# The update of the samples' matrix states moves from the mixer to GpSimd, beside the FFN and the experts

## The chip, the cores and the metric

The kernel runs on one core of a Trainium2 chip. Times are device microseconds of one execution of the whole program. Engines are named TensorE (PE in the rows), VectorE (DVE), ScalarE (ACT), GpSimd (POOL) and SyncE (SP, which here only issues weight loads).

## The reference, cut to what matters

It is one inference step of a two-layer decoder for a prompt of 256 tokens and for 8 samples of one new token each. A layer is a mixer (one input projection, an HGRN2 group with 4 heads of 128x128 state and an RG-LRU group, one output projection) and a channel mixer: a dense SwiGLU in layer 0, top-2-of-8 experts in layer 1. The part that the change touches is the state of the samples. For one token and each head the reference comes down to

```python
f = lb + (1 - lb) * sigmoid(fz)          # forget gate, one per key row
k = (1 - lb) * sigmoid(-fz)              # key
S_new[k_row, :] = f[k_row] * S[k_row, :] + k[k_row] * v[:]
o = q @ S_new
```

`S_new` is an output of the program (8 samples, 4 heads, 128x128, per layer: 2 MB). The output `o` is computed as `(q*f) @ S + (q.k) * v`, from the old state, so nothing after the mixer needs `S_new`.

## The kernel before, in words

Every engine has its own program, written in the order in which it runs; semaphores join them. There is no scheduler. All 264 tokens (256 and 8) are the columns of tiles, features are the partitions. Buffers share places by hand (`at(name, offset, ...)`).

Weights come in units of 1 MB (`raw`, 6 slots, loaded by SyncE when slot u-6 has been split). ScalarE rounds a unit to `w_hi` (`hi`, L487), VectorE makes the rest `w_lo` (`lo`, L788), each with 3 slots; TensorE multiplies three times per piece (`mm3`, L1358 to L1360). This pipeline runs through everything: 12 units of the input projection, 4 of the output projection, 33 of the FFN (11 steps of 3), and per expert 7 steps of 6 units.

In a mixer, after the input projection, the engines work on a chain: gates (L1450, L589), decay factors (L602, L607), then on VectorE `cum`, `zx`, `lev` (L1021, L1023, L1039), the scans (L1041), the copy of the heads' outputs from PSUM (L1048) and the samples' own term (L1049). From there, one branch goes on through the square (L628), sums on TensorE (L1508), Ln and Exp (L632, L633), `zf` (L1075) and the gating of four heads (L1077) to `m_hi` and `m_lo` (L622, L1069); the other is the RG-LRU's (L1054 to L1063), whose four chunks are merged first. The output projection takes the chunks in the order 4 to 7, 0 to 3, and VectorE adds each of its 8 columns of output to `xT` (L1093).

The samples' states: ScalarE issues the load of `hstate` (L555) behind the input projection, since it lies where `h_hi` and `h_lo` lie. TensorE reads it (L1486, 32 products of one column). GpSimd multiplies it by the forget gate (L412, eight instructions of 128x512). The value row of a sample has to reach all 128 partitions: GpSimd makes diagonal matrices of its high and low part (`v_diag`, L424, sixteen instructions), TensorE multiplies them by ones (`spread_value`, L1500, two matmuls per sample), and VectorE adds key times the PSUM row to the decayed state (`new_state`, L1033, four per sample). Two samples are handled before the output projection, and one behind each of its first six columns. GpSimd then stores the 2 MB (L428). `norm_hi` on ScalarE (L523) waits for that store before it writes `h_hi` of the next norm; in layer 1 VectorE waits for it before the router's work.

In the expert stage GpSimd only gathers the next expert's tokens (L449, an indirect DMA), once per expert.

Of the kernel before, what the change touches and what calls it, by code (L numbers as in the profile page):

```python
# [42 lines left out]
STATES_FIRST = 2  # L43
# [29 lines left out]
def trunk(nc, x_prompt, x_sample, state_hgrn, state_lru, state_conv, norm1_g, w_in, lower_bounds,  # L73
# [5 lines left out]
    with ctx:  # L79
# [14 lines left out]
        def end(name):  # L94
# [15 lines left out]
        small = at("small", end("rw"), [168])  # L110
# [21 lines left out]

        v_diag = [at("v_diag0", end("v_tok"), [2, HEADS, P], F32R),
                  at("v_diag1", end("key"), [2, HEADS, P], F32R)]
# [7 lines left out]
        vs = at("vs", end("outs_t"), [2, HEADS, NSAMPLE], F32R)  # L142
# [27 lines left out]
        rt = at("rt", HH, [16, 3, EXPERTS])  # L170
# [3 lines left out]
        y_rows = at("y_rows", end("hF"), [3, D])  # L174

        ps = ctx.enter_context(nc.psum_tensor("ps", [P, 8, 512], F32))
        h_dram = nc.dram_tensor("h_rows_scratch", [T, D], F32, kind="Internal").ap()

# [11 lines left out]
        tmp = small[:, 48:160]  # L190

# [22 lines left out]
        gelu_ready, vs_high, vs_split = sem("gelu_ready"), sem("vs_high"), sem("vs_split")  # L214
# [6 lines left out]
        st_landed, st_decayed, diag_ready = sem("st_landed"), sem("st_decayed"), sem("diag_ready")  # L221
        kv_done, st_new, st_stored = sem("kv_done"), sem("st_new"), sem("st_stored")
# [124 lines left out]
        def _(pool):  # L347
# [49 lines left out]
            for l in range(DEPTH):  # L397
# [17 lines left out]
                pool.wait_ge(fin_done, l + 1)  # L415
                pool.wait_ge(vs_split, l + 1)
                for b in range(NSAMPLE):
                    if b == 1:
                        pool.wait_ge(om_ready, l + 1)
                    if b >= 2:  # L420
                        pool.wait_ge(kv_done, NSAMPLE * l + b - 1)
                    for part in range(2):
                        v_b = vs[:, part, :, b:b + 1].bitcast(F32).broadcast_to([P, HEADS, P])
# [19 lines left out]
            pool.wait_ge(st_stored, 16 * DEPTH)  # L443
            pool.wait_ge(fin_stored, 16 * DEPTH)
            pool.wait_ge(rows_stored, 16 * (1 + 4 * DEPTH))
# [6 lines left out]

            pool.wait_ge(h_stored, 16 * 3)
            pool.wait_ge(idx_ready, 1)
            gather_rows()
            pool.wait_ge(blocks_ready, 1)
            nb = pool.value_load(blocks_i[0:1, 0:1], min_val=1, max_val=3)
            with pool.Fori(0, nb) as b:
                with pool.Fori(0, EXPERTS) as e:
                    it = b * EXPERTS + e  # L460
                    pool.wait_ge(idx_ready, it + 2)
                    pool.wait_ge(gathered, it * 2 + 2)
                    pool.sem_inc(gather_begun, 1)
                    gather_rows()
# [4 lines left out]
        def _(act):  # L469
# [1346 lines left out]
```

## Time and profile before

| | |
|---|---|
| runs | 1667.12, 1672.84, 1673.19 us; median 1672.84 |
| profiled execution | 1667.08 us, its span 1665.4 us |
| TensorE busy | 1551.2 us, mean granted clock 0.961 |
| VectorE busy | 1302.6 us |
| ScalarE busy | 963.2 us |
| GpSimd busy | 116.5 us |
| DMA | 438.9 MB, mean 264 GB/s |

The profile is of one execution. Busy shares are of the whole span; its stages are the first mixer (to about 208 us), the FFN (to 395), the second mixer (to 600), the router (to 630) and the experts (to 1640). PEclk is the clock that TensorE was granted, as a part of 2.4 GHz: 0.5 is 1.2 GHz.

### The profile page before, as it was taken

What the parts mean: (1) busy time and instruction counts of PE and PEld (TensorE: products, weight loads), DVE (VectorE), ACT (ScalarE), POOL (GpSimd) and SP (SyncE); (2) the same over time, 40 slices, a digit from 0 to 9 for tenths busy, and PEclk for the clock granted to TensorE, in tenths of its full rate; (3) what the DMA queues carried; (4) which work ended last, traced back from release to release, by engine and by line L of the source; (5) the groups of instructions that cost most, each with busy time, mean ns of one, the idle gap of its engine ahead of it and who ended that gap; (6) DMA issues with size and microseconds to landing.
All of it is one profiled execution on the core that took longest, in us unless ns stands there. A gap on an engine that the chain in (4) does not pass through costs nothing.

```text
span 1665.4 us, 23819 instructions
## 1 busy us (share of the span) xinstructions
PE 1551.2 (93%) x8538; PEld 1332.5 (80%) x8538; DVE 1302.6 (78%) x1244; ACT 963.2 (58%) x800; POOL 116.5 (7%) x104
## 2 busy tenths in 40 slices
PE   6986899999897677999999999999999999999996
PEld 5985799999897676888888888888888888888884
DVE  5786656666667747889889889889889889889886
ACT  4434343334534316677677677677677677677672
POOL 2024400000002610000000000000000000000000
PEclk9996999999999678999999999999999999999999
DMA  8451444445334036999999999999999999999990
GB/s 272 158 162 36 134 147 166 167 165 187 128 127 127 15 105 252 334 378 351 339 376 355 338 382 345 339 380 349 340 373 354 338 376 346 344 379 354 336 360 26
DMA packets 214524, 438.88 MB, mean 264 GB/s; under 512 B 7248, under 2 KB 62984, under 8 KB 214480
## 3 DMA queue, kind: packets, MB, share of 16 engines
q1 hardware_dynamic: 208176, 421.59, 71.1%
q0 software_dynamic: 3088, 10.14, 1.9%
q10 hardware_dynamic: 3216, 6.55, 1.3%
q8 instruction: 29, 0.48, 0.1%
q14 instruction: 15, 0.12, 0.0%
HBM read 431.29 MB, written 7.03 MB: 263 GB/s over the span
## 4 chain that ended last, share of the span: by engine, by line
PE 84%; DVE 9%; issue 3%; ACT 2%; DMA 1%; PEld 0%; DVEq 0%; ACTq 0%; SPq 0%; POOLq 0%; PEldq 0%
PE ps L1358 26%; PE ps L1360 25%; PE ps L1359 25%; DVE w_lo L788 2%; PE ps L1402 1%; PE ps L1675 1%; PE ps L1374 1%; DMA out_dram<-hstate 1%; DVE xc L1041 1%; PE ps L1647 1%; DVE xc L949 1%; PE ps L1635 1%; DVE zq L922 1%; DVE sc L937 0%; DVE lev L1077 0%
## 5 line engine op out<-in xcount | busy, mean ns | idle before, releaser
L788 DVE TENSOR_TENSOR w_lo<-raw,w_hi 128x2048 fp32r<-128x2048 f32 x401 | 913.7, 2292 | 189.0 <-ACT w_hi L487 186.6
L487 ACT ACTIVATE w_hi<-raw 128x2048 fp32r<-128x2048 f32 x401 | 762.7, 1917 | 357.9 <-PE ps L1360 207.8
L1358 PE MATMUL ps<-w_hi,xg 128*128 128x512 f32 x896 | 358.1, 400 | 9.9 <-DVE w_lo L788 9.9
L1360 PE MATMUL ps<-w_hi,xg 128*128 128x512 f32 x896 | 351.7, 392 | 0.0
L1359 PE MATMUL ps<-w_lo,xg 128*128 128x512 f32 x896 | 351.6, 392 | 0.0
L1358 PE MATMUL ps<-h_hi,w_hi 128*128 128x264 f32 x736 | 215.9, 293 | 25.1 <-DVE h_lo L815 17.0
L1360 PE MATMUL ps<-h_hi,w_lo 128*128 128x264 f32 x736 | 211.2, 287 | 0.0
L1359 PE MATMUL ps<-h_lo,w_hi 128*128 128x264 f32 x736 | 211.0, 287 | 0.0
L1358 PEld LDWEIGHTS ps<-w_hi,xg 128*128 128x128 f32 x896 | 168.8, 188 | 47.9 <-DVE w_lo L788 14.0
L1360 PEld LDWEIGHTS ps<-w_hi,xg 128*128 128x128 f32 x896 | 168.5, 188 | 37.4
L1359 PEld LDWEIGHTS ps<-w_lo,xg 128*128 128x128 f32 x896 | 169.0, 189 | 33.5
L1358 PE MATMUL ps<-w_hi,gT 128*128 128x512 f32 x448 | 179.4, 401 | 2.2 <-DVE gT L1275 2.2
L1359 PE MATMUL ps<-w_lo,gT 128*128 128x512 f32 x448 | 176.9, 395 | 0.0
L1360 PE MATMUL ps<-w_hi,gT 128*128 128x512 f32 x448 | 176.8, 395 | 0.0
L1358 PEld LDWEIGHTS ps<-h_hi,w_hi 128*128 128x128 f32 x736 | 140.9, 191 | 30.1 <-issue 29.2
L1359 PEld LDWEIGHTS ps<-h_lo,w_hi 128*128 128x128 f32 x736 | 141.7, 193 | 0.0
L1360 PEld LDWEIGHTS ps<-h_hi,w_lo 128*128 128x128 f32 x736 | 140.8, 191 | 0.0
L1358 PEld LDWEIGHTS ps<-w_hi,gT 128*128 128x128 f32 x448 | 84.0, 187 | 27.2 <-DVE w_lo L788 9.3
L1360 PEld LDWEIGHTS ps<-w_hi,gT 128*128 128x128 f32 x448 | 84.0, 187 | 20.4
L1359 PEld LDWEIGHTS ps<-w_lo,gT 128*128 128x128 f32 x448 | 84.1, 188 | 17.9
L449 POOL DMA_INDIRECT xrow<-h_rows_scratch,slot_token x9 | 18.7, 2082 | 966.7 <-DVE slot_token L1202 939.6
L727 ACT ACTIVATE gT<-ps 128x512 fp32r<-128x512 f32 x56 | 33.6, 599 | 75.4 <-PE ps L1675 75.4
(271 smaller groups left out, 1619.0 us busy)
## 6 DMA issues: line engine op xcount, KB each, us to landing
raw<-in_moe_w_dram SPq DMA_DIRECT2D x336, 1024.0 KB, 6.6
raw<-in_ffn_w_dram SPq DMA_DIRECT2D x33, 1024.0 KB, 5.4
raw<-in_w_in_dram SPq DMA_DIRECT2D x24, 1024.0 KB, 5.6
raw<-in_w_out_dram SPq DMA_DIRECT2D x8, 1024.0 KB, 4.9
out_dram<-hstate POOLq DMA_DIRECT2D x2, 2048.0 KB, 12.2
x_rows<-in_x_prompt_dram SPq DMA_DIRECT2D x1, 1024.0 KB
h_rows_scratch<-h_row ACTq DMA_DIRECT2D x2, 512.0 KB
out_dram<-y_rows ACTq DMA_DIRECT2D x2, 512.0 KB
```

Source lines behind the costliest of these rows:

```text
L449: pool.indirect_dma_start(xrow[:, :], None, h_dram[:, :], bass.IndirectOffsetOnAxis(slot_token[:, 0:1], 0)).then_inc(xrow_landed, 16)
L487: act.activation(w_hi[:, s, :], raw[:, r, :], ACT.Copy).then_inc(hi_made, 1)
L727: act.activation(gT[:, 0, :, :].rearrange("p j n -> p (j n)"), ps[:, 2, :], ACT.Copy).then_inc(gT_hi, 1)
L788: dve.tensor_tensor(w_lo[:, s, :], raw[:, r, :], w_hi[:, s, :].bitcast(F32), ALU.subtract).then_inc(split, 1)
L922: dve.tensor_tensor(qv[:, :, :, 1, :], qv[:, :, :, 1, :], wide(0), ALU.mult).then_inc(lev_ready, 1)
L949: link(dve.scalar_tensor_tensor(out=xc[:, j, 0:NPROMPT], in0=zx[:, j, tap:tap + NPROMPT], scalar=v(V_CW + 16 * l + 4 * tap + j), in1=xc[:, ...
L1041: link(dve.tensor_tensor_scan(xc[:, j, 0:NPROMPT], lev[1][:, j, 0:NPROMPT], lev[2][:, j, 0:NPROMPT], 0.0, ALU.mult, ALU.add))
L1358: pe.matmul(out, l_hi, r_hi, start=start, stop=False)
L1359: pe.matmul(out, l_hi, r_lo, start=False, stop=False)
L1360: return pe.matmul(out, l_lo, r_hi, start=False, stop=stop)
L1374: ins = pe.matmul(ps[:, NORM_BANK[n], 0:T], ones[:, :], sq[:, c, :], start=(c == 0), stop=(c == DC - 1))
L1402: ins = pe.matmul(ps[:, 4 + n % 4, P * h:P * h + P], left[:, h, P * c:P * c + P], right[:, h, P * rc:P * rc + P], start=True, stop=True)
```

## The change

In the mixer, GpSimd no longer decays states or makes diagonals, TensorE no longer spreads values and VectorE no longer updates states. Instead:

- TensorE transposes the samples' values to rows (8 x 512 in PSUM), ScalarE copies them to `vrow`, and GpSimd's queue stores them in DRAM (`v_dram`). ScalarE keeps the samples' keys and forget gates in `key_s` and `forget_s` (before, it made `vs`, and VectorE its low part).
- `vrow` lies where the heads' copy is written, so VectorE waits for that store before the copy.
- Layer 0: once the output projection is done, GpSimd loads the old states again to a place of their own (`hstate2`, free in the FFN). Each sample's value row is then read from DRAM into all partitions (`load_value`, 256 KB, three buffers), and GpSimd does three multiplications and additions of 128x512 per sample (`new_state`). The store follows the last one. ScalarE and VectorE wait for it when layer 1's mixer begins.
- Layer 1: `hstate` stays where it is (the router's tables `rt` have moved), and one sample is updated behind each expert's gather. The loop over the first block's experts is written out on GpSimd for this.
- `norm_hi(1)` waits for the state reads (`o_done`) and not for the store.

The operations on the states are in float32 on one engine, where the values came from two parts before.

```diff
-        vs = at("vs", end("outs_t"), [2, HEADS, NSAMPLE], F32R)
+        hstate2 = at("hstate2", end("ff_lo"), [NSAMPLE * HEADS, P])
+        vb = at("vb", end("y_f"), [3, HEADS, P])
...
@@ gpsimd, mixer
-                pool.wait_ge(st_landed, 16 * (l + 1))
-                for b in range(NSAMPLE):
-                    pool.wait_ge(st_read, NSAMPLE * l + b + 1)
-                    f_b = forget[:, :, NPROMPT + b:NPROMPT + b + 1].broadcast_to([P, HEADS, P])
-                    st = hstate[:, HEADS * b:HEADS * (b + 1), :]
-                    pool.tensor_tensor(st, st, f_b, ALU.mult).then_inc(st_decayed, 1)
...
-                        pool.tensor_tensor(v_diag[b % 2][:, part, :, :],
-                                           ident[:, None, :].broadcast_to([P, HEADS, P]), v_b,
-                                           ALU.mult).then_inc(diag_ready, 1)
-                pool.wait_ge(st_new, NSAMPLE * HEADS * (l + 1))
-                pool.dma_start(hgrn_sample[l].rearrange("b h k v -> k (b h) v"), hstate[:, :, :]
-                               ).then_inc(st_stored, 16)
+                pool.wait_ge(vrow_ready, l + 1)
+                pool.dma_start(v_dram[l], vrow[0:NSAMPLE, :]).then_inc(vrow_stored, 16)
...
+            def load_value(l, b):
+                pool.dma_start(vb[:, b % 3, :, :].rearrange("p h v -> p (h v)"),
+                               v_dram[l, b:b + 1, :].broadcast_to([P, HEADS * P])
+                               ).then_inc(vb_landed[b % 3], 16)
+            def new_state(l, b, st):
+                pool.wait_ge(vb_landed[b % 3], 16 * (per_layer * l + b // 3 + 1))
+                link(pool.tensor_tensor(own_v, own_v, wide(key_s), ALU.mult))
+                link(pool.tensor_tensor(own_st, own_st, wide(forget_s), ALU.mult))
+                link(pool.tensor_tensor(own_st, own_st, own_v, ALU.add))
+                if b + 3 < NSAMPLE:
+                    load_value(l, b + 3)
+                if b == NSAMPLE - 1:
+                    pool.dma_start(hgrn_sample[l].rearrange("b h k v -> k (b h) v"), st
+                                   ).then_inc(st_stored, 16)
...
+            mixer(0)
+            pool.wait_ge(y_done, DC)
+            pool.wait_ge(fin_stored, 16)
+            pool.wait_ge(rows_stored, 16 * 5)
+            pool.dma_start(hstate2[:, :, :], state_hgrn[0].rearrange("b h k v -> k (b h) v")
+                           ).then_inc(st_again, 16)
+            pool.wait_ge(st_again, 16)
+            values_begin(0)
+            for b in range(NSAMPLE):
+                new_state(0, b, hstate2[:, :, :])
+            mixer(1)
...
+            for e in range(EXPERTS):
+                gather_expert(e)
+                new_state(1, e, hstate[:, :, :])
@@ scalar
-                if n in (1, 3):
-                    act.wait_ge(st_stored, 16 * ((n + 1) // 2))
+                if n == 1:
+                    act.wait_ge(o_done, 1)
...
+                if l:
+                    act.wait_ge(st_stored, 16 * l)
...
+                    if u == SPLIT + 4:
+                        act.wait_ge(f_made, l + 1)
+                        act.activation(key_s, key[:, :, NPROMPT:T], ACT.Copy).then_inc(kf_ready, 1)
+                        act.activation(forget_s, forget[:, :, NPROMPT:T], ACT.Copy
+                                       ).then_inc(kf_ready, 1)
-                act.activation(vs[:, 0, :, :], zv[:, :, NPROMPT:T], ACT.Copy
-                               ).then_inc(vs_high, 1)
...
+                act.activation(vrow[0:NSAMPLE, :], ps[0:NSAMPLE, 2, :], ACT.Copy
+                               ).then_inc(vrow_ready, 1)
@@ vector
+                if l:
+                    dve.wait_ge(st_stored, 16 * l)
...
-                    for h in range(HEADS):
-                        st = hstate[:, HEADS * b + h, :]
-                        dve.scalar_tensor_tensor(
-                            out=st, in0=ps[:, 5 + b % 3, P * h:P * h + P],
-                            scalar=key[:, h, NPROMPT + b:NPROMPT + b + 1], in1=st,
-                            op0=ALU.mult, op1=ALU.add).then_inc(st_new, 1)
...
+                dve.wait_ge(vrow_stored, 16 * (l + 1))
                 link(dve.tensor_copy(heads[:, :, :], ps[:, 0:4, 0:T]))
@@ tensor
+                for h in range(HEADS):
+                    ins = pe.transpose(ps[0:NSAMPLE, 2, P * h:P * h + P], zv[:, h, NPROMPT:T],
+                                       ident[:, :])
                 ins.then_inc(v_turned, 1)
...
+                pe.wait_ge(vrow_ready, l + 1)
...
-                    for part in range(2):
-                        ins = pe.matmul(ps[:, 5 + b % 3, :], ones_r[:, :],
-                                        v_diag[b % 2][:, part, :, :].rearrange("p h v -> p (h v)"),
-                                        start=(part == 0), stop=(part == 1))
-                    ins.then_inc(kv_done, 1)
```

How the instructions stand on GpSimd in layer 0 before, from the gelu product (`zr`) on; `hstate` is the samples' state, `v_diag` the diagonals:

```order
L405 TENSOR_TENSOR zr<-zr,zf 128x1056 [waits gelu_sig]
L412 TENSOR_TENSOR hstate<-hstate,forget 128x512 [waits st_read,st_landed]
L412 TENSOR_TENSOR hstate<-hstate,forget 128x512 [waits st_read] x7
L424 TENSOR_TENSOR v_diag_80<-ident,vs 128x512 [waits vs_split,fin_done]
L424 TENSOR_TENSOR v_diag_80<-ident,vs 128x512
L424 TENSOR_TENSOR v_diag_81<-ident,vs 128x512 [waits om_ready]
```

The same place in the changed kernel, to the first sample's update; `hstate_110` is `hstate2`:

```order
L409 TENSOR_TENSOR zr<-zr,zf 128x1056 [waits gelu_sig]
L412 DMA v_rows_scratch<-vrow 8x512 [waits vrow_ready]
L414 DMA out_dram<-s_fin 128x4x128 [waits fin_ready]
L418 DMA out_dram<-outs_t 4x128 [waits rows_ready]
L466 DMA hstate_110<-in_state_hgrn_dram 128x32x128 [waits rows_stored,fin_stored,y_done]
L429 DMA vb<-v_rows_scratch 128x512 [waits kf_ready,vrow_stored,st_again]
L447 TENSOR_TENSOR vb<-vb,small 128x512 [waits vb_landed0]
L448 TENSOR_TENSOR hstate_110<-hstate_110,small 128x512 [waits pool_step]
L449 TENSOR_TENSOR hstate_110<-hstate_110,vb 128x512 [waits pool_step]
```

Between the gelu product and the end of the output projection, only DMA issues are left on GpSimd. VectorE in layer 0 before, from the gating of the heads on:

```order
L1077 SCALAR_TENSOR_TENSOR lev_74<-lev_74,vecT,zf 128x264 x3
L1069 TENSOR_TENSOR m_lo<-lev_74,m_hi 128x264 [waits m_hi_made] x4
L1033 SCALAR_TENSOR_TENSOR hstate<-ps,key,hstate 128x128 [waits st_decayed,kv_done]
L1033 SCALAR_TENSOR_TENSOR hstate<-ps,key,hstate 128x128 x3
L788 TENSOR_TENSOR w_lo<-raw,w_hi 128x2048 [waits hi_made]
L1089 COPY outs_t<-ps 80x128 [waits rows_turned]
```

And in the changed kernel:

```order
L1107 SCALAR_TENSOR_TENSOR lev_74<-lev_74,vecT,zf 128x264 x3
L1099 TENSOR_TENSOR m_lo<-lev_74,m_hi 128x264 [waits m_hi_made] x4
L828 TENSOR_TENSOR w_lo<-raw,w_hi 128x2048 [waits hi_made]
L1117 COPY outs_t<-ps 80x128 [waits rows_turned]
L1121 TENSOR_TENSOR xT<-xT,ps 128x264 [waits y_done] x4
```

The state updates between the low parts, and behind each addition to `xT`, are gone.

## Rows read from the trace of the kernel before

**Rows 1.** The page: a group of instructions, and two kinds of transfers (landing in us).
```profile
L788 DVE TENSOR_TENSOR w_lo<-raw,w_hi 128x2048 fp32r<-128x2048 f32 x401 | 913.7, 2292 | 189.0 <-ACT w_hi L487 186.6
...
raw<-in_moe_w_dram SPq DMA_DIRECT2D x336, 1024.0 KB, 6.6
...
out_dram<-hstate POOLq DMA_DIRECT2D x2, 2048.0 KB, 12.2
```

**Rows 2.** Stages: length, PE, PEld, DVE, ACT, POOL busy (x); clock, DMA share, GB/s.
```profile
112.00:165.00 53.00, 32.08 (x202) 28.69 (x200) 38.71 (x55) 25.34 (x40) 19.15 (x13) 0.75 0.32 99
165.00:195.00 30.00, 27.69 (x182) 26.14 (x183) 23.65 (x51) 8.45 (x9) 14.56 (x13) 0.87 0.20 62
...
210.00:395.00 185.00, 179.93 (x1446) 177.95 (x1446) 111.63 (x130) 71.44 (x56) 0.00 (x0) 0.99 0.50 166
...
630.00:1640.00 1010.00, 1000.40 (x4565) 812.84 (x4566) 878.90 (x585) 710.99 (x475) 17.68 (x8) 1.00 0.96 347
```

**Rows 3.** GpSimd: timeline (start, us), and the tile of diagonals (ns min/median/max, first and last start).
```profile
118.63 2.47 POOL L405 TENSOR_TENSOR zr<-zr,zf 128x1056 f32<-128x1056 f32 x1 [12.21 <-ACT zf L576]
141.84 12.27 POOL L412 TENSOR_TENSOR hstate<-hstate,forget 128x512 f32<-128x512 f32 x8 [20.74 <-PE ps L1486]
166.67 4.89 POOL L424 TENSOR_TENSOR v_diag<-ident,vs 128x512 fp32r<-128x512 f32 x4 [8.14 <-PE ps L1500]
...
L424 POOL TENSOR_TENSOR v_diag<-ident,vs x32: 1042/1050/1756, 154.1 to 582.5; 128x512 fp32r<-128x512 f32 x32
```

**Rows 4.** VectorE beside GpSimd's work, layer 0: timeline, and two lines of tile queries.
```profile
142.38 1.62 DVE L1021 TENSOR_TENSOR cum<-lev 128x1056 f32<-128x1056 f32 x1 [4.29 <-ACTq L609]
144.04 1.98 DVE L1023 SCALAR_TENSOR_TENSOR zx<-cum,zx 128x1056 f32<-128x1056 f32 x1
147.24 1.81 DVE L1039 TENSOR_TENSOR lev<-lev,zx 128x1056 f32<-128x1056 f32 x1 [1.22 <-ACT zx L617]
154.93 1.26 DVE L1048 COPY lev<-ps 128x1056 f32<-128x1056 f32 x1
156.48 1.08 DVE L1054 TENSOR_TENSOR xc<-vecT,lev 128x32 f32<-128x32 f32 x1
166.56 4.09 DVE L1077 SCALAR_TENSOR_TENSOR lev<-lev,vecT,zf 128x264 f32<-128x264 f32 x4
...
L1041 DVE TENSOR_TENSOR_SCAN xc<-lev,lev x8: 1352/1354/1418, 149.1 to 548.9; 128x256 f32<-128x256 f32 x8
...
L1069 DVE TENSOR_TENSOR m_lo<-lev,m_hi x8: 421/422/1272, 170.6 to 568.1; 128x264 fp32r<-128x264 f32 x8
```

**Rows 5.** VectorE where GpSimd is idle, layer 0: timeline.
```profile
123.56 0.21 DVE L967 TENSOR_TENSOR small<-vecT 128x32 f32<-128x32 f32 x1
132.09 1.25 DVE L1016 TENSOR_TENSOR zg<-zg,cum 128x1056 f32<-128x1056 f32 x1
204.79 1.30 DVE L809 SCALAR_TENSOR_TENSOR hF<-xT,vecT,rstd 128x264 f32<-128x264 f32 x3
```

**Rows 6.** TensorE in the second half of layer 0's mixer: timeline.
```profile
140.66 9.30 PE L1486 MATMUL ps<-zq,hstate 128*128 128x1 f32 x64
157.78 3.89 PE L1508 MATMUL ps<-zf,ones 128*128 128x264 f32 x8 [7.81 <-ACT zf L628]
171.90 0.39 PE L1358 MATMUL ps<-m_hi,w_hi 128*128 128x264 f32 x1 [2.02 <-DVE m_lo L1069]
```

**Rows 7.** The chain in layer 1's output projection: start, us, what.
```profile
577.51 0.46 PE ps L1500 x2
```

**Rows 8.** ScalarE at the norm behind layer 0's mixer: timeline.
```profile
207.43 1.05 ACT L523 ACTIVATE h_hi<-hF 128x264 fp32r<-128x264 f32 x3 [4.51 <-DMA out_dram<-hstate]
```

**Rows 9.** Waits in the expert stage, 700 to 1600: us in total, times, longest.
```profile
ACT w_hi L487 <- PE ps L1360: 187.4, 195, 1.6
DVE w_lo L788 <- ACT w_hi L487: 95.7, 137, 1.3
...
PEld ps L1358 <- DVE w_lo L788: 12.0, 36, 0.8
```

More of the change, by code:

```diff
@@ L109, in trunk @@
         rw = at("rw", end("gate_w"), [DC, EXPERTS])
-        small = at("small", end("rw"), [168])
+        small = at("small", end("rw"), [232])
         HH = end("small")
@@ L131, in trunk @@
         k_tok = at("k_tok", end("v_tok"), [2, HEADS, P])
-        v_diag = [at("v_diag0", end("v_tok"), [2, HEADS, P], F32R),
-                  at("v_diag1", end("key"), [2, HEADS, P], F32R)]
+        vrow = at("vrow", end("cum"), [HEADS * P])
         xc = at("xc", end("k_tok"), [HEADS, T])
@@ L213, in trunk @@
         q_ready = sem("q_ready")
-        gelu_ready, vs_high, vs_split = sem("gelu_ready"), sem("vs_high"), sem("vs_split")
+        gelu_ready, f_made, kf_ready = sem("gelu_ready"), sem("f_made"), sem("kf_ready")
+        vrow_ready, vrow_stored = sem("vrow_ready"), sem("vrow_stored")
+        vb_landed = [sem(f"vb_landed{i}") for i in range(3)]
         qk_done, st_read, lev_ready = sem("qk_done"), sem("st_read"), sem("lev_ready")
@@ L395, in _, with mixer @@
                            ).then_inc(rows_stored, 16)
-            for l in range(DEPTH):
+            def mixer(l):
                 pool.wait_ge(z_free, 4 + 24 * l + 20)
@@ L442, in _, with values_begin @@
                                rows(O_XRS, 32)).then_inc(rows_stored, 16)
[L443 to L445 removed]
+            def load_value(l, b):
+                pool.dma_start(vb[:, b % 3, :, :].rearrange("p h v -> p (h v)"),
+                               v_dram[l, b:b + 1, :].broadcast_to([P, HEADS * P])
+                               ).then_inc(vb_landed[b % 3], 16)
+            def values_begin(l):
+                pool.wait_ge(vrow_stored, 16 * (l + 1))
+                pool.wait_ge(kf_ready, 2 * (l + 1))
+                for b in range(3):
+                    load_value(l, b)
+            def new_state(l, b, st):
+                per_layer = len(range(b % 3, NSAMPLE, 3))
+                pool.wait_ge(vb_landed[b % 3], 16 * (per_layer * l + b // 3 + 1))
+                own_st = st[:, HEADS * b:HEADS * (b + 1), :]
+                own_v = vb[:, b % 3, :, :]
+                wide = lambda a: a[:, :, b:b + 1].broadcast_to([P, HEADS, P])
+                link(pool.tensor_tensor(own_v, own_v, wide(key_s), ALU.mult))
[6 more added lines that the diff above has]
+                                   ).then_inc(st_stored, 16)
             def gather_rows():
@@ L455, in _, with gather_expert @@
             gather_rows()
+            pool.wait_ge(y_done, 2 * DC + DC * FF_STEPS)
+            pool.wait_ge(st_read, NSAMPLE * DEPTH)
+            values_begin(1)
             pool.wait_ge(blocks_ready, 1)
             nb = pool.value_load(blocks_i[0:1, 0:1], min_val=1, max_val=3)
[L458 to L464, printed above, removed]
+            def gather_expert(it):
+                pool.wait_ge(idx_ready, it + 2)
+                pool.wait_ge(gathered, it * 2 + 2)
+                pool.sem_inc(gather_begun, 1)
+                gather_rows()
+            for e in range(EXPERTS):
+                gather_expert(e)
+                new_state(1, e, hstate[:, :, :])
+            with pool.If(nb > 1):
+                with pool.Fori(1, nb) as b:
+                    with pool.Fori(0, EXPERTS) as e:
+                        gather_expert(b * EXPERTS + e)
+            pool.wait_ge(st_stored, 16 * DEPTH)
             pool.wait_ge(xrow_landed, nb * (16 * EXPERTS) + 16)
@@ L1081, in mixer @@
                     merge_low(n)
-                for b in range(STATES_FIRST):
-                    new_state(b)
                 lo(ob + 3)
@@ L1490, in mixer @@
                 pe.sem_inc(o_done, 1)
-                def spread_value(b):
-                    pe.wait_ge(diag_ready, 2 * (NSAMPLE * l + b + 1))
-                    if b < 3:
-                        pe.wait_ge(o_root, l + 1)
-                    else:
-                        pe.wait_ge(st_new, HEADS * (NSAMPLE * l + b - 2))
-                    for part in range(2):
-                        ins = pe.matmul(ps[:, 5 + b % 3, :], ones_r[:, :],
-                                        v_diag[b % 2][:, part, :, :].rearrange("p h v -> p (h v)"),
-                                        start=(part == 0), stop=(part == 1))
-                    ins.then_inc(kv_done, 1)
                 pe.wait_ge(o_sq, l + 1)
@@ L1514, in mixer @@
                              ).then_inc(rows_turned, 1)
-                for b in range(STATES_FIRST):
-                    spread_value(b)
                 n0 = 0 if l == 0 else DC + DC * FF_STEPS
```

34 lines of the change are left out of this document (10 added, 24 removed).

## The prediction

> **What bounds the kernel now.** The page's costliest groups come first: splitting the weights into high and low halves, of which the low one (w_lo, VectorE) takes 2.29 us each, 401 times [rows 1], and the matmuls. Shares of the whole span mix stages with different limits, so the table by stage comes next [rows 2]. In the expert stage (630 to 1640 us) TensorE is busy 1000 of 1010 us, and in the FFN (210 to 395) 180 of 185: there it is the bound, at full clock. In the second half of a mixer (112 to 165) it is busy 32 of 53 us at a mean clock of 0.75, and waits for a chain of short VectorE and ScalarE work. So the change is worth what it takes out of the two mixers, less what it costs TensorE in the FFN and the expert stage.
>
> Then I put GpSimd's timeline [rows 3] beside VectorE's [rows 4]. GpSimd decays the states from 141.84 to 154.11 and makes the diagonals from 154.1 and again from 166.67. Exactly in these stretches VectorE is slow: a 128x32 multiply of two SBUF operands takes 1.08 us (L1054) against 0.21 us (L967), a 128x1056 one 1.62 and 1.81 us against 1.25 us, and a 128x264 scalar_tensor_tensor 4.09/4 = 1.02 us against 1.30/3 = 0.43 us [rows 4, 5]. The PSUM copy at L1048 keeps its 1.26 us in the same stretch. So GpSimd work holds up VectorE instructions that read two SBUF operands by up to one GpSimd instruction, whose shortest is 1.04 us [rows 3].
>
> The Trainium skill says the same as a mechanism (SBUF — State Buffer, "SBUF: two separate sides"): the pair is an exclusive lock for a whole instruction, and the loser blocks. The rows of the diagonals agree. By that rule every w_lo in the expert stage could also be blocked, which is rival A.
>
> **What goes from the mixer, per layer.** Both layers show the same durations (the eight scans of L1041 lie within 1352 and 1418 ns [rows 4]), so one layer is worked out and taken twice.
>
> Step 1, up to the heads' copy. L1021 goes from 1.62 to 1.25 and L1039 from 1.81 to 1.26: 0.92. L1023 has no undisturbed twin; four times the 0.43 of the quarter-size one is 1.7, the multiply of its size is 1.25; I take 1.35 of its 1.98: 0.63. The scans are the open one. They take 1.35 each beside decays that take 12.27/8 = 1.53 (1.04 when alone). Either a scan takes 1.35 by itself (gain 0), or the two engines take turns and a scan is as short as about 0.4 (gain 3.8 for four). I take 0.75, gain 2.4, since a neighbour that pushes a 0.2 us instruction to 1.08 will hardly leave these alone. L1049 gives another 0.15. Sum 4.1. The limit is what is late next: the matmuls that read the states end at 149.96 [rows 6] and the copy starts at 154.93 now, so no more than 4.9 can come from here; the step's range is 1.7 to 4.9.
>
> The Trainium skill (DVE: opcode table, instruction layouts, handler registers and perf-mode slots, "Datapath and trigger behaviour") has the built-in scan at half throughput; with VectorE's 0.96 GHz (the Trainium skill, Trainium Kernel Development and Optimization, "NeuronCore Architecture") that is 0.53 us of streaming for 256 columns, an estimate that would make the step some 4.5. No row shows an undisturbed scan.
>
> Step 2, L1054 and L1055, lose 0.8 to 0.9 each, but off the path: ScalarE's Ln needs the sums of squares of L1508, which run from 157.78 to 161.67 [rows 6] and hang on step 1 alone. I count 0 (at most 1.6).
>
> Step 3, gating the heads. Four L1077 go from 4.09 to about 1.75, and the first m_lo behind them from 1.27 to 0.42 [rows 4]: 2.34 + 0.85 = 3.2. TensorE waits 2.02 us for that m_lo, until 171.90 [rows 6]. Late next is TensorE's own first part (the transpose and 12 matmuls at half clock, about 3.1 us after o_root) against VectorE's 1.26 + 1.75 + 0.42 = 3.4 us from the same moment: they about meet, so the 3.2 are kept. Range 2 to 3.5.
>
> Step 4, the spread matmuls. Sixteen matmuls per layer go. Those of the first two samples lie before the first projection, in the time in which TensorE would wait anyway; six pairs stand between projections, 0.46 us each [rows 7]: 2.8. VectorE's eight times four updates lie beside the projection, which is TensorE's: 0, or a few tenths where an addition was late. The low weights of unit 3 (ScalarE, then VectorE) are due two columns later: covered.
>
> Step 5, layer 0 only. The first h_hi starts at 207.43, after 4.51 us of idle time that the 2 MB store ends [rows 8]; its input, the first hF of L809, starts at 204.79 and takes 0.43 [rows 5]. Without the store it starts at about 205.4: 2.0. In layer 1 the store's landing is waited for by VectorE's router work, and the logits are later: 0.
>
> Layer 0: 4.1 + 3.2 + 2.8 + 2.0 = 12.1. Layer 1: 10.1. Sum 22.2.
>
> **What it adds.** In the mixer: four transposes of 128x8, one PSUM copy of 8x512, two 128x32 copies on ScalarE (for one before, and VectorE's 128x32 subtraction goes), and an 8-row store on GpSimd's queue. The transposes and the copies lie before the gate matmuls; between 112 and 165 TensorE is idle for 21 us and ScalarE for 28 [rows 2], so I take 0, at most 1 us. VectorE's new wait for that store (before L1048, with the whole chain queued behind it) is for a transfer issued behind the gelu product, which ends at 121.1 [rows 3]; the state store took 12.2 us to land [rows 1], so it is there by 134, against 151 in the new timeline: 0. If that cover were gone, each us late would be a us lost.
>
> The new waits for the state store at the start of layer 1's mixer have ScalarE's and VectorE's whole mixer behind them. From about 190, GpSimd reads 2 MB (11 to 13 us), makes 24 instructions, each at worst behind one w_lo (1.04 + 2.3 = 3.3, 80 us in all), waits for a few broadcasts, and stores in 12: done by 315 at the latest, and the mixer begins near 383. 0.
>
> Port cost. GpSimd now runs 24 instructions in the FFN and 3 per expert. Each can hold up one w_lo by up to 1.04 us. In the expert stage, w_lo waits 95.7 us in 900 for ScalarE, and ScalarE waits 187 for TensorE; but weight loads wait for w_lo 36 times, 12.0 us in sum [rows 9]. So most units have room, at least one place in a step has none. In FFN, VectorE is busy only 112 of 185 us [rows 2]. Bounds: 0 and 24 x 1.04 = 25 us in either stage. The row nearest is that of the present waits (0.8 us at the longest), and the three instructions of an expert fall within about 10 us of its 1010/8 = 126: I take 0.3 per expert, 2.4, and 0.5 in the FFN.
>
> Transfers. The expert stage moves 347 GB/s with the DMA engines 96% busy, and gets 2 MB of broadcasts (0.25 MB per sample) and a 2 MB store more. A weight unit lands 6.6 us after issue, and ScalarE, who takes it, is never seen waiting for one [rows 1, 9]; with six slots and 1010/56 = 18 us for a round of six units there are several us of room, and 0.25 MB costs 0.7 us of transfer. Bounds 0 and 4 MB/347 GB/s = 12 us; I take 0.5, nearer to the wait rows.
>
> TensorE's clock: 165 to 195 had a mean of 0.87 [rows 2], that is 26% of 30 us at 1.2 GHz, or 3.9 us of work lost. The moment of rise will move. I take 0, plus or minus 2 per layer.
>
> **Sum.** 22.2 - 2.4 - 0.5 - 0.5 = 18.8. The profiled execution took 1667.1 us (its span 1665.4 and 1.7 around it), so the changed one would take 1648.3. The median shown is 1672.8, with one run at 1667.1 and one at 1673.2; for a median I add half of the 5.8 between profile and median: 1651.
>
> **The rivals.** A, the port turned round: GpSimd instructions delay w_lo where no room is, and the delay reaches TensorE. For it: the blocking in rows 4, and 12.0 us of existing waits. Against: w_lo stands idle 95.7 us in 900 [rows 9], some 12 per expert, and three instructions take 3.1 at most. It decides for slower when over 22.2/48 = 0.46 us of each of the 48 instructions reaches TensorE; at 0.8 it costs 38 and the time, from the same 1667.1 + 2.9 as above, is 1670 - 22 + 38 = 1686. Chance 0.06.
>
> B, the added 4 MB count in full, since the DMA engines are nearly always busy: 12 us, the gain is 22.2 - 2.9 - 12 = 7 and the time about 1663. Against: no wait for a landing. Chance 0.12.
>
> C, the slow VectorE instructions are so by themselves and GpSimd's presence is coincidence, or TensorE's state matmuls hold the chain: only steps 4 and 5 are left, 5.6 + 2.0, less the costs 3.4: 4 us, about 1666. Against: the 0.21 and 1.08 us of one shape. Chance 0.08.
>
> D, layer 1's mixer begins late because the states are not stored, for 20 us or more: the time would be about 1671 to 1680. It needs over 68 us beyond my worst case. Chance 0.02.
>
> My forecast: 0.72, with its own range of 1642 to 1660. Differences under 0.5% (8.4 us) can't be told from none. Faster than 1664.5: nearly all of the forecast, B mostly, some of C: 0.84. Within: 0.09. Slower: 0.07. The range that holds 0.8 is 1640 to 1668.
>
> **What would show it.** Right: the 128x32 multiply behind the heads' copy at 0.2 us, scans below 1 us, the four gating instructions below 0.5 us each, the first h_hi 0.6 us after the first hF, and the stage from the first state matmul to the end of the output projection some 10 us shorter in both layers. Costs: the mean of w_lo in the expert stage above 2.29 us, and the sum of waits for it above 12 us. Wrong: scans still at 1.35 us (then step 1 is 1.7), an expert longer than now by over a microsecond, or ScalarE waiting for a landing of raw.

## The result

| | median us | runs | ratio to before (95% interval) |
|---|---|---|---|
| before | 1672.3 | 1667.1 to 1673.2 (4) | 1 |
| changed | 1656.2 | 1652.6 to 1657.7 (4) | 0.9906 (0.9883 to 0.9928) |
| changed, measured again on another occasion | 1654.1 | 1651.0 to 1659.1 (5) | 0.9914 (0.9898 to 0.9929) |

The change makes the kernel 0.9% faster. The forecast was 1651 us with a range of 1640 to 1668, so direction and range hold; the gain was 16 us where about 22 against the median had been put down. The first profiled execution of the changed kernel took 1657.2 us (span 1655.4), 10 us less than the one before; the profiled execution of the second occasion took 1651.0 (span 1649.2). Below they are called the first and the second profile.

VectorE in layer 0's mixer after the change, its timeline (start, duration, engine, line, operation), which answers to [rows 4]:

```profile
143.11 1.26 DVE L1061 TENSOR_TENSOR cum<-lev 128x1056 f32<-128x1056 f32 x1 [4.29 <-ACTq L649]
144.41 1.26 DVE L1063 SCALAR_TENSOR_TENSOR zx<-cum,zx 128x1056 f32<-128x1056 f32 x1
146.88 1.26 DVE L1068 TENSOR_TENSOR lev<-lev,zx 128x1056 f32<-128x1056 f32 x1 [1.21 <-ACT zx L657]
148.17 2.87 DVE L1070 TENSOR_TENSOR_SCAN xc<-lev,lev 128x256 f32<-128x256 f32 x4
151.30 1.26 DVE L1078 COPY lev<-ps 128x1056 f32<-128x1056 f32 x1
152.70 0.20 DVE L1084 TENSOR_TENSOR xc<-vecT,lev 128x32 f32<-128x32 f32 x1
162.78 1.71 DVE L1107 SCALAR_TENSOR_TENSOR lev<-lev,vecT,zf 128x264 f32<-128x264 f32 x4
164.41 1.46 DVE L1099 TENSOR_TENSOR m_lo<-lev,m_hi 128x264 fp32r<-128x264 f32 x4
```

Every instruction with two SBUF operands is short now: a scan takes 0.69 us where it took 1.35, the small multiply 0.20 where it took 1.08, four gatings 1.71 where they took 4.09. The copy from PSUM takes what it took, 1.26.

TensorE and ScalarE at the two places that [rows 6] and [rows 8] showed, also layer 0:

```profile
154.00 3.89 PE L1524 MATMUL ps<-zf,ones 128*128 128x264 f32 x8 [3.44 <-ACT zf L668]
...
164.89 0.59 PE L1383 MATMUL ps<-m_hi,w_hi 128*128 128x264 f32 x1 [0.29 <-DVE m_lo L1099]
...
196.22 1.17 ACT L556 ACTIVATE h_hi<-hF 128x264 fp32r<-128x264 f32 x3 [2.46 <-DVE hF L849]
```

The wait for the first m_lo has shrunk from 2.02 to 0.29 us, so TensorE and VectorE do meet there; h_hi waits for hF and no longer for the store.

Then the cost. In the expert stage, VectorE (first fence) and GpSimd (second) around the first update:

```profile
681.97 2.29 DVE L828 TENSOR_TENSOR w_lo<-raw,w_hi 128x2048 fp32r<-128x2048 f32 x1
684.17 0.68 DVE L1295 TENSOR_TENSOR ex_g<-ex_silu,ps 128x512 f32<-128x512 f32 x1
684.81 9.93 DVE L828 TENSOR_TENSOR w_lo<-raw,w_hi 128x2048 fp32r<-128x2048 f32 x3
```

```profile
685.16 1.06 POOL L447 TENSOR_TENSOR vb<-vb,small 128x512 f32<-128x512 f32 x1
686.30 2.99 POOL L448 TENSOR_TENSOR hstate<-hstate,small 128x512 f32<-128x512 f32 x1
689.37 3.22 POOL L449 TENSOR_TENSOR hstate<-hstate,vb 128x512 f32<-128x512 f32 x1
```

Three w_lo take 9.93 us instead of 6.85, about one GpSimd instruction (1.06 us) longer each; two of the GpSimd instructions (2.99 and 3.22 us) each wait for a w_lo in turn. TensorE notices. Waits over 700 to 1600 us, total, times, longest, to be held against [rows 9]:

```profile
DVE w_lo L828 <- ACT w_hi L520: 79.6, 115, 1.3
PEld ps L1383 <- DVE w_lo L828: 19.2, 50, 0.8
```

The idle time before w_lo fell from 95.7 to 79.6 us, and TensorE's waits for it rose from 12.0 to 19.2.

To see where the time went, I take the start of VectorE's reciprocal in each of the five norms as marks. In us between them ("changed" is the first profile, "changed again" the second):

| stretch | before | changed | changed again |
|---|---|---|---|
| layer 0's mixer (norm 0 to 1) | 180.98 | 171.45 | 171.71 |
| end of norm 1, FFN (1 to 2) | 213.71 | 213.41 | 211.60 |
| layer 1's mixer (2 to 3) | 181.91 | 171.96 | 170.89 |
| router and experts (3 to 4) | 1053.35 | 1062.68 | 1058.50 |

The mixers gave 9.5 + 10.0 us and the removed store wait some 2 more (in the second row); FFN, router and experts took part of it back. One expert, from gather to gather as a mean of seven, takes (1565.07 - 682.82)/7 = 126.04 us (126.07 in the second profile) against (1577.60 - 700.47)/7 = 125.30 before. The gathers of the second and the last expert, before (first fence) and changed (second):

```profile
700.47 2.22 POOL L449 DMA_INDIRECT xrow<-h_rows_scratch,slot_token  x1 [77.98 <-DVE slot_token L1202]
...
1577.60 2.21 POOL L449 DMA_INDIRECT xrow<-h_rows_scratch,slot_token  x1 [123.11 <-DVE slot_token L1202]
```

```profile
682.82 2.32 POOL L458 DMA_INDIRECT xrow<-h_rows_scratch,slot_token  x1 [78.02 <-DVE slot_token L1227]
...
1565.07 2.33 POOL L458 DMA_INDIRECT xrow<-h_rows_scratch,slot_token  x1 [116.23 <-DVE slot_token L1227]
```

### The profile page after: what moved, and what is told of

It reads as the page before. It is cut to its first block, busy times and chain, and to the rows that moved or that the text cites. A ratio compares the mean times of both kernels' runs of the same rounds, so it can differ in the third digit from the quotient of the medians.

```text
span 1655.4 us, 23666 instructions
## 1 busy us (share of the span) xinstructions
PE 1551.0 (94%) x8514; PEld 1326.4 (80%) x8514; DVE 1296.8 (78%) x1178; ACT 964.3 (58%) x804; POOL 165.3 (10%) x123
## 4 chain that ended last, share of the span: by engine, by line
PE 76%; DVE 12%; issue 7%; ACT 4%; DMA 1%; DVEq 0%; ACTq 0%; SPq 0%; POOLq 0%
PE ps L1383 23%; PE ps L1384 22%; PE ps L1385 22%; DVE w_lo L828 6%; PE ps L1427 1%; ACT w_hi L520 1%; PE ps L1399 1%; PE ps L1686 1%; PE ps L1658 1%; DVE rstd L846 1%; DVE xc L992 1%; PE ps L1646 1%; DVE zq L965 1%; DVE sc L980 0%; DVE hF L849 0%
## 5 line engine op out<-in xcount | busy, mean ns | idle before, releaser
L828 DVE TENSOR_TENSOR w_lo<-raw,w_hi 128x2048 fp32r<-128x2048 f32 x401 | 941.7, 2365 | 174.7 <-ACT w_hi L520 171.8
L1383 PE MATMUL ps<-w_hi,xg 128*128 128x512 f32 x896 | 360.0, 402 | 11.5 <-DVE w_lo L828 10.1
L1385 PEld LDWEIGHTS ps<-w_hi,gT 128*128 128x128 f32 x448 | 84.4, 188 | 20.6
```

Of the source, the lines that this page charges most:

```text
L828: dve.tensor_tensor(w_lo[:, s, :], raw[:, r, :], w_hi[:, s, :].bitcast(F32), ALU.subtract).then_inc(split, 1)
L1383: pe.matmul(out, l_hi, r_hi, start=start, stop=False)
L1385: return pe.matmul(out, l_lo, r_hi, start=False, stop=stop)
```

## The experiments

### GpSimd's updates left out of the expert stage

```diff
-                link(pool.tensor_tensor(own_v, own_v, wide(key_s), ALU.mult))
+                if l == 0:
+                    link(pool.tensor_tensor(own_v, own_v, wide(key_s), ALU.mult))
...
```

> The changed kernel without the three GpSimd instructions per sample in the expert stage (layer 1's new states are not computed; the value broadcasts and the 2 MB store stay). Theory port: the 0.7 us that each expert is longer than before come from these instructions holding up w_lo, so an expert falls from 126.0 to 125.3 us, the mean of w_lo in the stage to 2.29 us, and the profiled time by 5 to 7 us. Theory traffic: the broadcasts take the time, an expert stays at 126.0 us and the profiled time is unchanged.

Measured: one run, 1646.7 us. An expert takes (1556.95 - 679.84)/7 = 125.30 us, exactly as before, and router and experts 1052.26. The waits, same window and columns as above:

```profile
DVE w_lo L829 <- ACT w_hi L521: 96.1, 139, 1.3
PEld ps L1384 <- DVE w_lo L829: 12.0, 36, 0.8
```

Back to the 12.0 of before. The port theory holds for the experts. The whole is 10.5 us under the first profile, where 5 to 7 were expected, and 4.3 under the second: 2.2 of the 10.5 lie in the router and 1.7 in a spell at the lower clock in the last expert, of which more below.

### The transfers left out of the expert stage

```diff
-                if b + 3 < NSAMPLE:
+                if l == 0 and b + 3 < NSAMPLE:
...
-            values_begin(1)
+            link(pool.memset(vb[:, :, :, :], 0.0))
```

> The changed kernel without the value broadcasts and the store of the states in the expert stage (buffers set to zero once instead; layer 1's new states are wrong and not stored), with all GpSimd updates. Theory port: an expert stays at 125.9 to 126.0 us; at most 1 us is won in all, part of it where the first gather lands 0.6 us later than before. Theory traffic: an expert falls to 125.3 us and the last stretch (from the last gather to the end) from 90.3 to about 88 us.

Measured: one run, 1650.1 us. An expert takes (1558.22 - 676.13)/7 = 126.01 us. With updates and no transfers the loss is all there; with transfers and no updates it is gone. The two runs together refute rival B for the experts. The whole is 7.1 us under the first profile, where at most 1 was expected, and 0.9 under the second; most of the 7.1 lies in the FFN, the router and layer 1's mixer, which the edit does not touch. The last stretch, from the last gather to the end, came out at 90.1 us without the 2 MB store, and with it at 90.3 (first profile) and 88.7 (second). The run without the store and the first profile both hold a spell of 3.4 us at 1.2 GHz there, worth 1.7 us, the second profile none; without it they are 88.4, 88.6 and 88.7, so the store costs 0.3 us at most.

It is not without effect, though: ScalarE does wait for weights behind it. Second profile, same window and columns:

```profile
ACT w_hi L520 <- DMA raw<-in_moe_w_dram: 4.6, 5, 2.0
```

The five waits stand between 1583 and 1599, behind the store's issue at 1570.93. Five of the runs have such waits behind this store (1.2 to 5.5 us); the first profile has none, nor have the kernel before, the run without transfers and the versions further down that issue the store 36 us or more later in the last expert.

### GpSimd multiplications put back into the mixer

```diff
+                pool.wait_ge(fin_done, l + 1)
+                pool.wait_ge(st_read, NSAMPLE * l + 1)
+                for b in range(12):
+                    link(pool.tensor_tensor(dummy[:, 0, :, :], ident[:, None, :].broadcast_to(...),
+                                            key_s[:, :, 0:1].broadcast_to(...), ALU.mult))
+                pool.wait_ge(o_root, l + 1)
+                for b in range(4):
+                    link(...)
```

> The changed kernel with 16 GpSimd multiplications of 128x512 per layer put back into the mixer, twelve behind the first state read and four behind o_root, writing to a buffer nobody reads. Theory port: VectorE is slow again: scans 1.35 us instead of 0.72, the 128x32 multiply behind the heads' copy about 1 us instead of 0.20, the four gatings about 4.1 us instead of 1.7; from the first of these instructions to the start of the fifth chunk's matmul some 5 to 7 us longer per layer, the whole 10 to 13 us longer. Rival (the VectorE instructions sped up for another reason, such as no PSUM or semaphore traffic of the spreads): they stay as in the changed kernel and the time too.

Measured: one run, 1677.4 us. The stretches of the mixers take 180.24 and 181.66 us, again as before the change (180.98, 181.91). VectorE's timeline, layer 0:

```profile
149.73 5.58 DVE L1080 TENSOR_TENSOR_SCAN xc<-lev,lev 128x256 f32<-128x256 f32 x4
...
157.48 0.97 DVE L1095 TENSOR_TENSOR xc<-xc,lev 128x32 f32<-128x32 f32 x1
...
167.33 4.75 DVE L1117 SCALAR_TENSOR_TENSOR lev<-lev,vecT,zf 128x264 f32<-128x264 f32 x4
```

The scans return to 5.58 us to the hundredth. The gatings are slower than they ever were (4.75 against 4.09), with four GpSimd instructions in a row beside them; so this run shows the mechanism, and its total is not a measurement of each step. GpSimd instructions whose result nobody reads cost 18 to 19 us in the two mixers, and the whole is 20 us longer than the first profile, where 10 to 13 were expected. In layer 0 the heads' copy comes 4.3 us later, the gating and the first m_lo take 3.0 more, and the output projection, of which more runs at the lower clock, takes 1.1 more.

### GpSimd writes in the same places

Against the run before (first of its two places):

```diff
-                    link(pool.tensor_tensor(dummy[:, 0, :, :], ...))
+                    link(pool.memset(dummy[:, :, :, :], 0.0))
...
```

> The same places as in the run with multiplications put back, but GpSimd memsets of 128x1024 (16 per layer), which write and read nothing. Theory read side: VectorE instructions with two SBUF operands stay fast (scans 0.72, gatings 1.7 for four) and the time stays within 1 us of the changed kernel's profile. Theory any GpSimd access: as slow as with the multiplications, 10 us longer in all.

Measured: one run, 1652.8 us, 4.4 under the first profile and 1.9 above the second; mixers 171.15 and 171.89 us, as in the changed kernel. VectorE's timeline (first fence) with GpSimd's memsets (second) beside it, layer 0:

```profile
147.60 2.87 DVE L1078 TENSOR_TENSOR_SCAN xc<-lev,lev 128x256 f32<-128x256 f32 x4
...
152.36 0.19 DVE L1093 TENSOR_TENSOR xc<-xc,lev 128x32 f32<-128x32 f32 x1
152.58 0.47 DVE L1095 COPY outs<-xc 128x32 f32<-128x32 f32 x1
153.09 0.95 DVE L1096 COPY outs<-xc 128x4 f32<-128x4 f32 x1
```

```profile
141.98 12.04 POOL L417 MEMSET dummy<- 128x1024 f32 x12 [20.13 <-PE ps L1523]
```

Beside instructions that only write, operations with two SBUF operands keep their 0.69 and 0.19 us, so it is GpSimd's reading that holds them up. Copies from SBUF to SBUF are another matter: 0.95 us where the changed kernel has 0.17.

### ScalarE's small copies moved

```diff
-                    if u == SPLIT + 4:
-                        act.wait_ge(f_made, l + 1)
...
+                act.wait_ge(f_made, l + 1)
+                act.activation(key_s, key[:, :, NPROMPT:T], ACT.Copy).then_inc(kf_ready, 1)
```

> ScalarE's two 128x32 copies (samples' keys and gates) moved from the middle of the input projection to behind the vrow copy. In the changed kernel everything from the gelu work on stands 0.6 us later than before in layer 0 (100.88 against 100.28). Theory copies: they sit in the weight pipeline's way, and this start falls back to 100.3 us, 0.6 us per layer and about 1.2 us in all. Rival (code or semaphore differences elsewhere): it stays at 100.9.

Measured: one run, 1653.9 us; the gelu work starts at 100.76, not at 100.3. The guess falls: over the runs of this document with the copies in their old place it starts anywhere from 100.17 to 102.16, which is spread between executions.

### The updates put where VectorE has a gap

```diff
+                if l == 0:
+                    pool.wait_ge(ff_split, b + 1)
+                    ... the three instructions
+                else:
+                    s = b * EX_STEPS + 3
+                    pool.wait_ge(gT_split, START + s + 1)
+                    link(pool.tensor_tensor(own_v, own_v, wide(key_s), ALU.mult))
+                    pool.wait_ge(gT_split, START + s + 2)
+                    link(pool.tensor_tensor(own_st, own_st, wide(forget_s), ALU.mult))
+                    pool.wait_ge(gT_split, START + s + 3)
+                    link(pool.tensor_tensor(own_st, own_st, own_v, ALU.add))
```

> The updates stay on GpSimd, but each waits for a place where VectorE does not want the port: in the expert stage one instruction per step, released when the low part of gT is made (VectorE then idles 1.26 us for w_hi); in the FFN one sample per step, released by the low part of ff (VectorE then adds PSUM columns). Theory port: an expert takes 125.3 to 125.4 us instead of 126.0, the FFN stage 186.6 to 187.5 instead of 188.5, 6 to 8 us in all. Rival (the cost is the number of GpSimd instructions or their transfers, not their place): 126.0 as before.

Measured: one run, 1642.5 us. An expert takes (1552.85 - 675.70)/7 = 125.31 us, the marks of norm 1 and 2 are 210.87 apart (213.41 and 211.60 in the changed kernel), router and experts take 1052.19. GpSimd's first update, and VectorE on both sides of it, w_lo of the fifth unit last:

```profile
686.28 1.05 POOL L455 TENSOR_TENSOR vb<-vb,small 128x512 f32<-128x512 f32 x1 [8.27 <-DVE gT L1310]
```

```profile
685.44 0.68 DVE L1310 TENSOR_TENSOR gT<-ps,gT 128x512 fp32r<-128x512 f32 x1
687.40 6.83 DVE L838 TENSOR_TENSOR w_lo<-raw,w_hi 128x2048 fp32r<-128x2048 f32 x3 [1.27 <-ACT w_hi L530]
```

The instruction ends at 687.33, 0.07 us before VectorE starts. Nothing was removed from the changed kernel; each layer's 24 instructions only stand elsewhere: in the expert stage 10.6, 27.7 and 44.8 us behind the start of the gather, where they stood 2.3, 3.5 and 6.6 us behind it. (In the FFN the first sample's second and third instruction still meet a w_lo, 3.02 and 3.22 us; the other samples fit.)

### Both edits, and the changed kernel again

> Both edits together (updates in VectorE's gaps, ScalarE's copies late). Port and copies theories: about 8 us under the changed kernel, ratio to the kernel before 0.984 to 0.987. If neither holds: as the changed kernel, 0.990.

> The changed kernel again, in the rounds of the improved version, so that the two are compared on one chip. Expected 0.990 of the kernel before, as first measured, with 0.3% of spread between runs whose granted clock differs.

Measured: both edits 1643.9 us (5 runs, 1642.8 to 1644.6), ratio 0.9844 (0.9831 to 0.9857); the changed kernel 1654.1 (5 runs, 1651.0 to 1659.1), ratio 0.9914. The gain over the changed kernel is 10 us, more than the 8 expected.

### The gaps alone, timed

> The version with the updates in VectorE's gaps alone, timed. If ScalarE's copies cost nothing, as their own run says, it has the time of the version with both edits, 1643.9 us and ratio 0.984; if they do, 1 us more.

Measured: 1645.2 us (5 runs, 1643.5 to 1648.4), ratio 0.9847 (0.9834 to 0.9860). Not to be told from the version with both edits. These two are the best kernels here, some 26 us under the one before.

### The same, but where there is no room

Against the version with the updates in the gaps:

```diff
-                    pool.wait_ge(gT_split, START + s + 1)
+                    pool.wait_ge(hi_made, EX_BASE + 9 + RAW * (b * EX_STEPS + 3))
...
```

> As the version with the updates in the gaps, one instruction per step, but in the expert stage each is released when ScalarE has made w_hi of the step's fifth unit, which is when VectorE wants the port for the w_lo that TensorE has least room for. Theory port and room: each costs TensorE 0.3 to 0.9 us, so an expert takes 126.2 to 128 us, longer than with the three instructions in a row behind the gather (126.0). Rival (one instruction per step is harmless wherever it stands, only several in a row add up): 125.3 us.

Measured: one run, 1654.9 us; an expert takes (1562.28 - 678.75)/7 = 126.22 us, 0.91 more than in the gaps, or 0.30 per instruction: at the low end, and a little worse than the three in a row (126.04 and 126.07). GpSimd's timeline shows who wins:

```profile
690.58 3.08 POOL L455 TENSOR_TENSOR vb<-vb,small 128x512 f32<-128x512 f32 x1 [9.50 <-ACT w_hi L530]
```

3.08 us: VectorE had started the critical w_lo (690.46) and GpSimd waited it out, then held up the next one. So the place decides; spacing alone does not help.

### The spread matmuls put back

```diff
+                        if c < 6:
+                            for part in range(2):
+                                pe.matmul(ps[:, 5 + c % 3, :], ones_r[:, :], m_hi[:, 0:2, 0:256],
+                                          start=(part == 0), stop=(part == 1))
```

> The changed kernel with two matmuls of 512 columns put back behind each of the first six columns of the output projection, in both layers (their result is used by nobody). Theory of step 4: they stand on TensorE's path, 0.46 us a pair, so from the second to the third norm (and from the first to the second) 2.8 us longer than in the changed kernel: 174.7 instead of 171.9 for the second. Rival (the projection waits for VectorE's additions or for weights anyway): under 1 us.

Measured: one run, 1657.7 us; norm 2 to 3 takes 172.34 us, 0.4 more than the changed kernel's 171.96, and norm 0 to 1 takes 172.82, 1.4 more. Neither theory had it: six pairs cost about half of 2.8. (The whole is 3.8 to 6.7 us longer than the memset run, the run with late copies and the second profile: 1652.8, 1653.9 and 1651.0. Some 1.5 us of that stands between norm 1 and 2, where the lower clock behind layer 0's mixer lasts 6.8 us instead of 3.4.) The additions to xT show it in layer 1, changed kernel:

```profile
562.03 0.43 DVE L1121 TENSOR_TENSOR xT<-xT,ps 128x264 f32<-128x264 f32 x1 [0.58 <-PE ps L1385]
565.47 0.43 DVE L1121 TENSOR_TENSOR xT<-xT,ps 128x264 f32<-128x264 f32 x1 [3.01 <-PE ps L1385]
568.37 0.43 DVE L1121 TENSOR_TENSOR xT<-xT,ps 128x264 f32<-128x264 f32 x1 [2.47 <-PE ps L1385]
571.81 0.43 DVE L1121 TENSOR_TENSOR xT<-xT,ps 128x264 f32<-128x264 f32 x1 [3.02 <-PE ps L1385]
```

The columns are 3.44 and 2.90 us apart in turn. At the end of a unit of two columns TensorE waits for its own last result (`y_done`) before it frees the unit, and that makes the 0.54 us between the two distances. TensorE's first matmul of the next unit:

```profile
568.63 0.36 PE L1383 MATMUL ps<-m_hi,w_hi 128*128 128x264 f32 x1 [0.31 <-PE ps L1385]
```

A pair that stands there fills that pause; only the pair in the middle of a unit adds its 0.47 (in the run with pairs the distances were 3.44 and 3.37). Three pairs of six, 1.4 us, which is what layer 0 shows. Layer 1 shows only 0.4 because the clock hides the rest: in the changed kernel the first 2.7 us of its projection run at 1.2 GHz (mean clock 0.94 over it), in the run with pairs none (1.00).

## Why the prediction was right, and where it was off

The mechanism held and was shown; the costs were mis-sized.

**Step 1** (4.1 us, range 1.7 to 4.9) held. The heads' copy comes 50.42 us after the start of the gelu work where it came 54.65 after it: 4.2. The scans, the open term, take 0.69 us (0.75 was taken). For them the prediction had an estimate from the Trainium skill's half throughput (DVE: opcode table, instruction layouts, handler registers and perf-mode slots, "Datapath and trigger behaviour"), 0.53 us of streaming. The trace agrees: m_lo (264 columns), ff_lo (528) and L1061 (1056) take 0.43, 0.71 and 1.26 us, that is 1.04 ns a column and 0.16 us besides, and with twice the time per column 256 columns come to 0.69. The run with multiplications in the mixer shows that GpSimd's presence was the cause of the 1.35.

**Step 2** held: Ln still starts when the sums of squares end (154.00 + 3.89 = 157.89, Ln at 157.92).

**Step 3** (3.2) held: from the gating's first start to the first m_lo's end it was 5.3 us and is 2.05. Rival C is out by this and by the run with multiplications.

**Step 4** (2.8) was right in mechanism and twice too large: half of the pairs stood in the `y_done` pause. That the output projection nevertheless became 2.1 and 1.9 us shorter (from the first m_lo's end to the last addition, 26.65 to 24.51 and 26.67 to 24.78) is those 1.4 plus less time at 1.2 GHz: in layer 1 before, the granted clock was still 0.62 in 570 to 573, 2.5 to 5.5 us after TensorE resumed; now it is 1.00 from 3 us after. That help from the clock, which the prediction had put at nothing, is luck as far as this step's number goes.

**Step 5** (2.0) held: last addition to first h_hi took 8.94 us and takes 6.88.

**The mixers together** gave 9.5 + 2.1 in layer 0 and 10.0 in layer 1, 21.6 us, where 22.2 was forecast.

**The port cost** is the term that was mis-sized. For the experts 0.3 each had been taken, 2.4 in all; it is 0.74, as the two runs without updates or transfers and the gaps show, and 5.9 for eight. The row I chose by was the longest present wait; the right question was how the three instructions fall on the units. They come in a row behind the gather, and one after the other they hold up three w_lo. In the FFN 0.5 was taken. There the time from the last addition of layer 0 to the gelu work of layer 1 (less the 2.0 of step 5) grew by 1.9 us in the first profile, and shrank by 0.6 in the second, and from norm 1 to 2 the eight profiles with the updates in a row have two sizes, 211.3 to 211.6 us twice and 213.4 to 215.1 six times: in the six, the low parts of ff in the first two steps are both caught by GpSimd instructions (1.28 to 1.77 us for 0.71), in the two neither is. In the first profile, and then in the second:

```profile
212.59 1.51 DVE L1139 TENSOR_TENSOR ff_lo<-ff_g,ff_hi 128x528 fp32r<-128x528 f32 x1 [0.71 <-ACT ff_hi L699]
```

```profile
213.44 0.71 DVE L1139 TENSOR_TENSOR ff_lo<-ff_g,ff_hi 128x528 fp32r<-128x528 f32 x1 [0.71 <-ACT ff_hi L699]
```

With the updates in the gaps it is 210.9 to 211.3 in all four. So the updates in a row cost the FFN some 0.5 or some 2.5 us more than in the gaps, by chance of phase. Where exactly the phase is decided was not tested, and no run leaves the FFN's updates out.

**The transfers** (0.5) cost nothing that can be seen in an expert. TensorE waits 6.2 to 7.0 us for the first gather's rows where it waited 6.4, with three broadcasts issued behind that gather, and 6.0 without them: 0.2 to 1 us. The stretch from the first gather to the second is 0.8 to 1.7 us longer in all changed versions, also without transfers; the rest of that is open. One sign that the prediction named for being wrong did appear, ScalarE waiting for a landing of raw (4.6 us in the second profile); the last stretches show no cost of it beyond 0.3 us.

**The clock** was given 2 us per layer either way and showed up most clearly behind the mixers. From norm 3 to the first gather the first profile of the changed kernel takes 22.87 us, as before (22.85), at a mean clock of 0.59; the second takes 20.71, at 0.67, and so do all the other runs (20.6 to 20.7) but the one with the multiplications put back (24.05). Then the last expert: first profile, the windows' columns as in [rows 2]:

```profile
1600.00:1641.80 41.80, 37.71 (x157) 28.19 (x155) 25.82 (x25) 21.18 (x23) 0.00 (x0) 0.96 0.33 130
```

The 0.96 is one spell of 3.4 us at 1.2 GHz, 59 us behind the last gather, 1.7 us of work; the second profile has 1.00 there. The spell stands in six of the eight profiles whose updates meet w_lo in the expert stage (five in a row, and the one without room), and in none of the five where they don't, the kernel before included. So it may well be a cost of the updates too, but what brings it was not tested. The router, this spell and the FFN's phase (1.8) are nearly all of the 6 us between the two profiles.

**The sum in profiles.** The mixers and step 5 gave 21.6 us in the first profile and 22.3 in the second, and the whole is 9.9 and 16.1 us shorter. So 11.7 and 6.2 us were lost elsewhere, where the prediction had 3.4. From the first gather to norm 4 the loss is 9.3 and 7.3 us (of which the versions with gaps keep about 1), in the FFN 1.8 and 0; the router gave 0 and 2.1. Against the prediction's 1648.3 for a profiled execution stand 1657.2 and 1651.0. That the medians differ by 16 us where the first profiles differ by 10 comes from the kernel before, whose profiled execution lies 5.2 us under its median, while the changed one's lies 1.0 above; the 2.9 us that the prediction added for this made up for part of the mis-sized cost, and that is luck.

**Rival A** was the right worry with the wrong size: 5.9 us in the experts, 0.5 or 2.5 in the FFN and 1.7 if the spell is counted, 6.4 to 10.1 us of 48 instructions, 0.13 to 0.21 each, where 0.46 would have undone the gain. **Rival B** is refuted, **C** too, and **D**: the last FFN-stage update ended at 249.2 and its store lands long before 383.

## What to carry to other kernels

Work on an engine that is never the bound still costs, when it reads SBUF while VectorE runs operations with two SBUF operands: look for one shape that has two durations. Where VectorE idles such work cost nothing here (an expert took 125.31 us with it and 125.30 without), and VectorE's copy from PSUM kept its 1.26 us beside it. A semaphore that VectorE raises at the start of its gap was enough to put it there; spaced out but misplaced, it cost slightly more than in one lump (126.22 against 126.04). Before counting an instruction removed from the critical engine in full, look whether it stood in a pause that stays.

## What the runs showed that was not expected

- VectorE and GpSimd take turns with whole instructions: beside GpSimd multiplies (1.04 us alone) a 0.69 us scan takes 1.35 us, and a w_lo of 2.29 us up to 3.57. The Trainium skill describes an exclusive lock (SBUF — State Buffer, "SBUF: two separate sides"); all runs agree.
- A GpSimd memset leaves two-operand instructions alone (0.19 us) but holds up SBUF-to-SBUF copies of 4 columns, 0.95 us for 0.17.
- The gather's issue on GpSimd takes 2.1 to 2.4 us beside VectorE's splitting (w_lo) and 1.06 in the router, where VectorE only writes zeros beside it (a memset of 0.91 us).
- The two versions with the updates in the gaps spread by 1.7 and 4.9 us over five runs, the changed kernel by 8.2; whether that is the order or chance, five runs don't tell.
